# The last three of sixty DRAM-to-DRAM copies move from ScalarE's DMA queue to SyncE's, behind the residual rows

## The reference

```
proj = einsum('btd,de->bte', x, w_in)
q, k, v, g_att, gb, gc, hh, g_conv = split(proj)
att = dilated_attention(q, [k_past, k], [v_past, v]) * silu(g_att)
z   = gb * conv3(gc * hh) * silu(g_conv)
y   = layer_norm(alpha * x + concat(att, z) @ w_out, ln_g, ln_b)
outputs: y, new keys and values of the prompt, the shifted caches, new conv state
```

## Time and profile before

| | us |
|---|---|
| median of 3 runs | 360.97 (359.77 to 361.14) |
| the profiled execution, on the device | 360.34 |
| its span, first to last instruction | 358.5 |
| TensorE busy | 348.7 (97%) |
| VectorE busy | 202.1 (56%) |
| ScalarE busy | 117.4 (33%) |
| packets of q1 and of q10, share of 16 DMA engines | 50.8% and 47.6% |

### The profile page before, as it was taken

One profiled execution on the slowest core, in us unless ns is written; L12 is line 12 of the kernel. 1 busy time (PEld: TensorE's weight loads), 2 busy tenths in 40 slices (PEclk: granted clock), 3 DMA queues, 4 the chain that ended last, 5 costly groups with the idle time before them and its releaser, 6 DMA issues.

```text
span 358.5 us, 7719 instructions
## 1 busy us (share of the span) xinstructions
PE 348.7 (97%) x3280; PEld 311.6 (87%) x3280; DVE 202.1 (56%) x381; ACT 117.4 (33%) x233; POOL 11.6 (3%) x28
## 2 busy tenths in 40 slices
PE   8999999999999999999999999999999999899992
PEld 6998888899989888999988889998879988688782
DVE  3724528764145558541446484613546598886774
ACT  4623324352153323421433333214441824330000
POOL 0000000000100000001000000000000004000000
PEclk9999999999999999999999999999999999999998
DMA  8999999999999999999999999999999999999991
GB/s 293 399 429 415 417 415 418 416 423 418 419 421 417 417 413 388 403 420 395 401 416 414 421 419 419 424 423 419 419 414 415 415 402 321 404 345 370 350 324 67
DMA packets 34836, 141.06 MB, mean 393 GB/s; under 512 B 3441, under 2 KB 3825, under 8 KB 32753
## 3 DMA queue, kind: packets, MB, share of 16 engines
q1 hardware_dynamic: 18338, 73.20, 50.8%
q10 hardware_dynamic: 16464, 67.37, 47.6%
HBM read 135.80 MB, written 71.86 MB: 579 GB/s over the span
## 4 chain that ended last, share of the span: by engine, by line
PE 82%; DMA 6%; DVE 5%; SPq 4%; ACT 1%; issue 0%; DVEq 0%; ACTq 0%
PE pj_a L1153 9%; PE pj_b L1153 9%; PE pj_b L1155 8%; PE pj_a L1155 8%; PE pj_a L1154 8%; PE pj_b L1154 8%; DMA wo_raw<-in_w_out 6%; PE sc L1310 4%; PE sc L1346 4%; PE px L1258 3%; PE po L1290 2%; PE pt L1276 2%; SPq L374 2%; SPq L303 2%; PE px L1503 2%; PE px L1504 2%
## 5 line engine op out<-in xcount | busy, mean ns | idle before, releaser
L1153 PE MATMUL pj_b<-x_hi,w_hi 128*128 128x288 f32 x248 | 75.1, 303 | 0.7 <-DVE mix L908 0.7
L1153 PE MATMUL pj_a<-x_hi,w_hi 128*128 128x288 f32 x248 | 75.7, 305 | 0.0
L1154 PE MATMUL pj_a<-x_lo,w_hi 128*128 128x288 f32 x248 | 73.2, 295 | 0.0
L1154 PE MATMUL pj_b<-x_lo,w_hi 128*128 128x288 f32 x248 | 73.1, 295 | 0.0
L1155 PE MATMUL pj_b<-x_hi,w_lo 128*128 128x288 f32 x248 | 73.0, 294 | 0.0
L1155 PE MATMUL pj_a<-x_hi,w_lo 128*128 128x288 f32 x248 | 72.9, 294 | 0.0
L785 DVE TENSOR_TENSOR w_lo<-w_raw,w_hi 128x1024 fp32r<-128x1024 f32 x30 | 36.7, 1223 | 32.3 <-ACT w_hi L472 32.3
L472 ACT CAST w_hi<-w_raw 128x1024 fp32r<-128x1024 f32 x30 | 31.4, 1047 | 69.2 <-DMA w_raw<-in_w_tiles 45.3
L1153 PEld LDWEIGHTS pj_a<-x_hi,w_hi 128*128 128x128 f32 x248 | 46.5, 187 | 6.8 <-issue 6.2
L1153 PEld LDWEIGHTS pj_b<-x_hi,w_hi 128*128 128x128 f32 x248 | 46.5, 187 | 3.1 <-issue 1.1
L1155 PEld LDWEIGHTS pj_b<-x_hi,w_lo 128*128 128x128 f32 x248 | 46.7, 188 | 0.0
(11 more groups left out here) (169 smaller groups left out, 452.5 us busy)
## 6 DMA issues: line engine op xcount, KB each, us to landing
k_buf<-in_k_used SPq DMA_DIRECT2D x16, 1280.0 KB, 15.5
v_buf<-in_v_used SPq DMA_DIRECT2D x40, 512.0 KB, 19.8
out_k_used_out<-in_k_used ACTq DMA_DIRECT2D x16, 1280.0 KB, 18.9
out_v_used_out<-in_v_used ACTq DMA_DIRECT2D x20, 1024.0 KB, 16.6
w_raw<-in_w_tiles SPq DMA_DIRECT2D x30, 512.0 KB, 12.8
out_k_rest_out<-in_k_rest ACTq DMA_DIRECT2D x12, 1024.0 KB, 12.6
out_v_rest_out<-in_v_rest ACTq DMA_DIRECT2D x12, 1024.0 KB, 13.1
wo_raw<-in_w_out SPq DMA_DIRECT2D x8, 512.0 KB, 21.8
```

The costliest lines, as they stand in the source:

```text
L1153: nc.tensor.matmul(out, w_hi[:, w], x_hi[:, c], start=(k == 0), stop=False)
L1154: nc.tensor.matmul(out, w_hi[:, w], x_lo[:, c], start=False, stop=False)
```

## The change

Three copies of used values (each 256 rows of 4 KB, 1 MB) leave ScalarE's program, where they stood behind the square roots of token tiles 0, 1 and 2. SyncE issues the same three, with the same rows and the same split over 16 engines, right behind the five residual loads and ahead of its first wait for `ln_done`. They count on a semaphore of their own, and SyncE's last wait takes in both. Nothing else is changed.

```
+LATE_COPIES = 3
...
+        late_copied = sem("late_copied")
...
             for t in range(QT + 1):
                 rows = P if t != SAMPLE_AT else NS
                 sp.dma_start(x_res[0:rows, t * 1024:(t + 1) * 1024], d["x_rows"][y_rows(t), :]).then_inc(res_in[t], 16)
+            for s in range(V_PIECES // 2 - LATE_COPIES, V_PIECES // 2):
+                rows = slice((V_PIECES * (NPAIR - 1) + 2 * s) * P, (V_PIECES * (NPAIR - 1) + 2 * s + 2) * P)
+                sp.dma_start(d["v_used_out"][rows, :].rearrange("(r a) n -> a r n", a=16),
+                             d["v_used"][rows, :].rearrange("(r a) n -> a r n", a=16)).then_inc(late_copied, 16)
             for t in range(QT):
                 sp.wait_ge(ln_done, t + 1)
...
-            sp.wait_ge(copied, 16 * (2 * REST_ROWS + NPAIR * (K_PIECES + V_PIECES // 2)))
+            sp.wait_ge(copied, 16 * (2 * REST_ROWS + NPAIR * (K_PIECES + V_PIECES // 2) - LATE_COPIES))
+            sp.wait_ge(late_copied, 16 * LATE_COPIES)
...
-            copies = iter(range(2 * REST_ROWS + NPAIR * (K_PIECES + V_PIECES // 2)))
+            copies = iter(range(2 * REST_ROWS + NPAIR * (K_PIECES + V_PIECES // 2) - LATE_COPIES))
...
                 nc.scalar.activation(std[0:rows, :], rstd[0:rows, :], ACT.Sqrt).then_inc(ln_sqrt, 1)
-                if t < 3:
-                    copy_next()
```

## The result

The changed kernel is slower: 364.00 us against 360.62 us (medians of 20 runs each, in turn on one chip), ratio 1.0079 with a 95% interval of 1.0061 to 1.0097. That is +2.8 us, between +2.2 and +3.5; the two medians themselves are 3.4 us apart. The forecast was 361.4 with a range up to 364.6, and +0.4 us for the change.

A forecast was written before the change was run, and what follows sets the result against it. TensorE was taken to bound the output stage, busy 41.20 of 41.30 us. Terms 0 + 0 + 0 + 0.4 + 0 gave +0.4 us on the median of 360.97, so 361.4 us, range 359.8 to 364.6.

The forecast's parts named there:

- The likeliest case: Whole kernel: +0.1 to +1.7 us, first store landing within 328.6 to 338.4; chance 0.42.
- What bounds the kernel and what is free: Output stage: TensorE bounds it, busy 41.20 of 41.30 us; VectorE's store waits of 3.42 and 1.09 us cost nothing.
- The limit of 38.88 us: VectorE at tile 4: a start up to 349.58, with the stage beginning at 310.70, costs nothing.
- Removed from ScalarE: 0: ScalarE's three issues taken out: their time was hidden under VectorE's statistics, so gain 0.
- Half the traffic is q1's: DMA queues when both are full: q1 gets half, 179 GB/s, between 166 and 208.
- The first store lands at 335.0: Store of tile 0 behind three copies in q1: lands at 335, between 328.6 and 337.6; up to 336.5 costs nothing.
- count from the last landing: First store: last residual tile lands at 315.5, then 3.67 MB take 20.5 us, to 336.0.
- The two queues carry 358 GB/s: Two queues of copies in the output stage together: 358 GB/s, bounds 333 and 415.
- The third store lands 9.0 us after its issue, and at 351.2 at the latest, when the copies end: Store before tile 4: issued 340.94, lands 349.94, tile 4 starts at 350.0; loss 0.4 us, between 0 and 1.7.
- ScalarE's issues stand no longer: 0: ScalarE's four remaining early copy issues: cost 0; above, tile 0 1.5 us late and the first root 0.4 us.
- The rival that was slower: First store lands so late behind q1's copies that VectorE, then TensorE, is late: 362.8 to 368 us; chance 0.18.
- The rule of turns: DMA engines alternate queues by packet; a fresh store lands well before 349.58, making the 0.4 us 0; the sum kept 9.0.

The follow-up runs named there:

- experiment 1: Changed kernel with five slots of y_t in place of two, so no tile waits for a landed store; ratio 0.9997 to the kernel before.
- experiment 3: Changed kernel with five slots of y_t and ScalarE's four copies moved behind the first two square roots; ratio 0.9987 to the kernel before.
- experiment 4: Changed kernel with SyncE's three copies left out altogether, their output rows not written; ratio 0.9995 to the kernel before.
- experiment 5: Changed kernel with one copy in SyncE's queue, the other two with ScalarE behind its roots of tiles 0 and 1; ratio 1.0001 to the kernel before.
- experiment 9: Kernel before with five slots of y_t, so neither VectorE wait for a landed store is left; ratio 1.0009 to the kernel before.
- experiment 2: Changed kernel with ScalarE's four copies between the mixed tiles' splits moved behind the first two square roots; ratio 1.0068 to the kernel before.
- 7: Changed kernel with SyncE's three copies issued behind the first store of y instead of ahead of the loop; ratio 1.0374 to the kernel before.
- 6: Changed kernel with five copies in SyncE's queue, adding the two behind the last mixed tile's split; ratio 1.0458 to the kernel before.
- experiment 10: Changed kernel with two copies in SyncE's queue, the third with ScalarE behind its root of tile 0; ratio 1.0098 to the kernel before.
- experiment 8: Kernel of experiment 2 with the first store of y issued by GpSimd on a third queue; ratio 1.0000 to the kernel before.
- experiment 12: Kernel of experiment 8, unedited, run again for a second profile; one execution at 359.07 us.
- experiment 11: Changed kernel, unedited, run again for a second profile; one execution at 362.38 us.

## Why the prediction was partly right

The time lay in the range, and the mechanism was the one that it described. The likeliest case, a loss of 0.1 to 1.7 us that measures as no change, did not come true; the +2.8 us lies where I had put a chance of 0.20. By its steps:

- *What bounds the kernel and what is free.* Right. Five slots in the kernel before change nothing (1.0009), and 3.15 MB fewer copies change nothing (0.9995). The limit of 38.88 us from the stage's first matmul to tile 4 sorts most of the cases. In experiments 1, 3, 4, 5 and 9 tile 4 began 35.1 to 37.7 us after it and the interval of the ratio held 1; in the changed kernel it was 40.8 and 41.1, in experiment 2 42.1, in 7 and 6 50.9 and 53.4, and all were slower. Two kernels it does not sort by their profiles: experiment 10 (38.98 us in its fastest execution, ratio 1.0098) and experiment 8 (40.3 us in its slowest execution, ratio 1.0000, and 35.7 in experiment 12).
- *Removed from ScalarE: 0.* Right: experiment 4.
- *Half the traffic is q1's.* Right: 1.61 against 1.61 MB from 318 to 328.
- *The first store lands at 335.0.* This term was mis-sized, and it is the step that failed. With the stage's start taken off (1.35 us) the store landed at 337.5, and in experiment 11 at 337.8, where 336.5 is the last that costs nothing. The miss has three parts. The working's own count from the last landing gave 336.0, and I took 335, toward the count by bytes (332.0): 1.0 us in both profiles. The last residual tile, behind which that count begins, took 14.8 and 15.8 us to land where 13.8 was carried over, and the count began 0.5 and 1.8 us later. From that landing to the store's there were 21.6 and 20.5 us where 20.5 was worked out: 1.1 and 0 us.
- *The two queues carry 358 GB/s.* Too high: the value was the mean of six favourable microseconds of one queue, and over 314 to 326 that same queue carried 337. Two queues of copies carried 322 from 318 to 328, and 331 over the longest such stretch (318 to 346 in experiment 6). From the last residual tile's landing to the third copy's (317.3 to 336.5) 3.15 MB took 19.3 us, 163 GB/s for q1, where I had put the slow end at 166. By the landings, as the bullet before has it, this cost the forecast at most 1.1 us.
- *The third store lands 9.0 us after its issue, and at 351.2 at the latest, when the copies end.* The first half held (8.0 us in both profiles), but the cap did not quite: ScalarE's last copy landed at 354.9, or 353.6 without the 1.35, and in experiment 11 at 351.9. The store landed at 352.76 (351.4 without the 1.35) and at 351.73, and tile 4 started 0.1 us later, where the working gave 350.0. Most of that is the first store's lateness handed on, since the third store was issued 2.5 and 2.8 us later than the 340.94 of the working; its shorter landing gave 1.0 us back.
- *ScalarE's issues stand no longer: 0.* The zero was right at the end and wrong on the way. The pair took 6.93 and 7.19 us where I had argued that it would see the same queue as before. It does not: the pair stood for 3.58 and 3.83 us with no copy of SyncE's issued ahead of it (experiments 4 and 7), and for 6.67 with one (experiment 5). VectorE was 3.9 us late at tile 0 (5.26 less 1.35) and TensorE stood for 0.31 us. The rest went into VectorE's idle before tile 2, which the working had named as the cover. Its upper bound for the first root leaves out the 1.1 us of ScalarE's work between the two pairs, from 312.56 to 313.64: it should read 328.4, and 1.5 us instead of 0.4. Experiments 1 and 2 show that this is not the loss: with the long issues and without the landing waits there is none, and without the long issues and with the waits nearly all of it stays.
- *The rival that was slower.* Its mechanism, the queue order, is what happened, in a milder form: TensorE was not late for tile 4, and it was to decide at a landing later than 338.4, where the store landed at 337.5 to 337.8 on that scale. The half per cent was passed all the same. The third store, which is issued later when the first lands later, was the one that tile 4 waited for: VectorE was free at 351.78 and idled 1.07 us.
- *The rule of turns* of the Trainium skill ("DMA: Bandwidth & Descriptors", section "Queues, rings and completion order"). Taken alone, it would let a store on an idle queue be served at the next turn. A third queue took 10.5 and 14.6 us (experiments 12 and 8), and SyncE's own queue, idle at the time, 9.0, 8.9 and 9.2 us (before, experiments 5 and 7). Here the measurements decide against the rule taken alone.

The two profiles account for +1.7 and +2.0 us of the +2.8, whose interval starts at +2.2. (Tile 4 was 1.9 and 2.2 us late by the working's limit, which is 0.2 us too early: with no idle in the tile VectorE reached the `sc` quarter 2.17 us after its start, where the working has 5.05 - 2.70 = 2.35.) The rest is scatter of single executions or a loss that no profile caught; it was not settled.

## What to carry to other kernels

In every profile here with three or five copies ahead of it on its queue the first store landed only behind the last of them, in experiment 2 although it was issued 17 us after that copy. So a bulk copy on a queue can be a wait for the small stores that follow: ask what is issued next on that queue, and who waits for its landing. A buffer with two slots turns that landing into an engine's wait; more slots took the loss away (0.9997), as did a third queue for the store (1.0000), and moving ScalarE's issues did not (1.0068). Count a moved DMA at the rate of the mixture that it makes, not of the one that it leaves.

## What the runs showed of the hardware that was not expected

- Two queues of copies from DRAM to DRAM carried no more together than one: 322 GB/s from 318 to 328 in the changed kernel and 331 from 318 to 346 in experiment 6. One queue of copies carried 337 from 314 to 326 in the kernel before, and 350 with a little store traffic from 334 to 346. Loads beside copies reached 415. The DMA packets of the kernel before from 314 to 326, and of experiment 6 from 318 to 346:

```profile
DMA packets 1048, 4.05 MB, mean 337 GB/s; under 512 B 63, under 2 KB 63, under 8 KB 1047
```

```profile
DMA packets 2415, 9.28 MB, mean 331 GB/s; under 512 B 150, under 2 KB 150, under 8 KB 2415
...
q10 hardware_dynamic: 1210, 4.66, 50.6%
q1 hardware_dynamic: 1205, 4.62, 49.6%
```

- A store that is issued on a queue with nothing in it still took about 9 us to land (9.0, 8.9, 9.2) while the other queue was full of copies, and 10.5 and 14.6 us on a third queue beside two full ones. Part of it is a late start: in the kernel before, with the store issued at 322.06, q1 moved one packet from 322 to 326 and 143 from 326 to 331.
- Issuing one DMA held ScalarE for 9.33 us (experiment 10, from 321.98); its longest in the output stage before was 4.13 us. A queue drained at half speed does not explain it: from 322 to 330 q10 moved 2.26 MB and q1 0.37 MB. The reason is open.
